# Gate and up rows of an expert side by side in one slot, multiplied as 512 columns

## What is computed

```python
def hier_moe(h, w_rg, b_rg, w_re, b_re, w1, w3, w2):
    """Top-1 group, then top-2 experts inside the chosen group; weight = p_group * p_expert."""
...
    comb = jnp.sum(jax.nn.one_hot(eid, N_EXPERTS, dtype=jnp.float32) * wts[..., None], axis=1)
    act = jax.nn.silu(jnp.einsum("nd,edf->nef", xt, w1)) * jnp.einsum("nd,edf->nef", xt, w3)
    act = act * comb[:, :, None].astype(act.dtype)
    y = jnp.einsum("nef,efd->nd", act, w2)
    return y.reshape(bsz, s, d)
```

## Time and profile before

| | |
|---|---|
| time, median of 3 runs (lowest to highest) | 917.99 us (917.68 to 918.61) |
| span of the profiled execution, first to last instruction | 914.1 us |
| PE (matmul) busy | 877.1 us, 96% |
| PEld (weight load) busy | 814.0 us, 89% |
| DVE busy | 625.9 us, 68% |
| ACT busy | 482.0 us, 53% |
| chain that ended last | PE 80%, DVE 13%, ACT 4% |
| HBM traffic over the span | 170 GB/s |

### The profile page before, as it was taken

The page is one execution under the profiler, slowest core; times in us unless marked ns, Lnnn a source line. Parts: engine busy times, 40 slices in busy tenths (PEclk is TensorE's granted clock), DMA queues, the critical chain, the costliest instruction groups (busy, mean ns, idle before and its releaser), DMA issues.

```text
span 914.1 us, 16487 instructions
## 1 busy us (share of the span) xinstructions
PE 877.1 (96%) x7196; PEld 814.0 (89%) x7196; DVE 625.9 (68%) x755; ACT 482.0 (53%) x576; POOL 44.5 (5%) x66
## 2 busy tenths in 40 slices
PE   5999999998988999999999999989999999999997
PEld 4998898998878999999979788989989999999986
DVE  5979477698938855478885986995466555455564
ACT  6557713657426744367774744565545543443463
POOL 6000060000000000000000000131000000000000
PEclk9999999999988999999999999999999999999999
DMA  9746210423107974579954544351454665555521
GB/s 268 264 157 203 88 49 4 139 93 139 47 1 301 380 272 162 187 269 365 356 195 139 184 139 138 98 191 51 169 184 150 211 204 184 184 185 186 183 92 46
DMA packets 88889, 156.73 MB, mean 171 GB/s; under 512 B 7417, under 2 KB 61169, under 8 KB 84849
## 3 DMA queue, kind: packets, MB, share of 16 engines
q1 hardware_dynamic: 88272, 155.42, 49.1%
q10 hardware_dynamic: 544, 0.26, 0.1%
HBM read 154.62 MB, written 1.05 MB: 170 GB/s over the span
## 4 chain that ended last, share of the span: by engine, by line
PE 80%; DVE 13%; ACT 4%; issue 2%; DMA 1%; POOL 0%; SPq 0%; DVEq 0%; POOLq 0%
PE ps L1043 9%; PE ps L1046 9%; PE ps L1045 9%; PE ps L1061 8%; PE ps L1063 8%; PE ps L1062 8%; DVE w_lo L1777 4%; PE ps L1485 4%; PE ps L1483 4%; PE ps L1484 4%; PE ps L1251 3%; PE ps L1555 2%; PE ps L1557 2%; PE ps L1556 2%; ACT w_hi L559 2%
## 5 line engine op out<-in xcount | busy, mean ns | idle before, releaser
L1777 DVE TENSOR_TENSOR w_lo<-raw,w_hi 128x2048 fp32r<-128x2048 f32 (+2 forms) x147 | 334.3, 2280 | 139.3 <-ACT w_hi L559 138.1
L559 ACT ACTIVATE w_hi<-raw 128x2048 fp32r<-128x2048 f32 (+2 forms) x147 | 277.5, 1892 | 76.4 <-PE ps L1063 27.5
L1043 PE MATMUL ps<-h_hi,w_hi 128*128 128x256 f32 x768 | 219.6, 286 | 5.9 <-DVE h_lo L1787 3.3
L1045 PE MATMUL ps<-h_lo,w_hi 128*128 128x256 f32 x768 | 217.2, 283 | 0.0
L1046 PE MATMUL ps<-h_hi,w_lo 128*128 128x256 f32 x768 | 217.2, 283 | 0.0
L1043 PEld LDWEIGHTS ps<-h_hi,w_hi 128*128 128x128 f32 x768 | 147.1, 192 | 8.7 <-issue 3.9
L1045 PEld LDWEIGHTS ps<-h_lo,w_hi 128*128 128x128 f32 x768 | 147.2, 192 | 0.4
L1046 PEld LDWEIGHTS ps<-h_hi,w_lo 128*128 128x128 f32 x768 | 147.1, 192 | 0.0
L1061 PE MATMUL ps<-w_hi,h_hi 128*128 128x512 f32 (+1 forms) x240 | 94.5, 394 | 0.5 <-DVE h_lo L2183 0.5
L1063 PE MATMUL ps<-w_hi,h_lo 128*128 128x512 f32 (+1 forms) x240 | 93.3, 389 | 0.0
L1062 PE MATMUL ps<-w_lo,h_hi 128*128 128x512 f32 (+1 forms) x240 | 93.2, 388 | 0.0
(11 more groups left out here) (435 smaller groups left out, 1350.5 us busy)
## 6 DMA issues: line engine op xcount, KB each, us to landing
raw<-in_w_in SPq DMA_DIRECT2D x36, 1024.0 KB, 5.1
raw<-in_w_exp_up SPq DMA_DIRECT2D x16, 1024.0 KB, 4.9
raw<-in_w_exp_down SPq DMA_DIRECT2D x16, 1024.0 KB, 4.9
raw<-in_w_exp_gate SPq DMA_DIRECT2D x15, 1024.0 KB, 4.9
raw<-in_w_ffn_gate SPq DMA_DIRECT2D x11, 1024.0 KB, 5.2
raw<-in_w_ffn_up SPq DMA_DIRECT2D x11, 1024.0 KB, 5.2
raw<-in_w_ffn_down SPq DMA_DIRECT2D x11, 1024.0 KB, 4.8
raw<-in_w_out SPq DMA_DIRECT2D x8, 1024.0 KB, 5.0
```

The costliest lines, as they stand in the source:

```text
L559: act.activation(w_hi[:, j % SPL, 0:kt * n], raw[:, j % RAW, 0:kt * n], ACT.Copy).then_inc(w_high, 1)
L1043: pe.matmul(o, hi[:, k, cols], a_hi[:, k, :], start=(k == 0 and (whole or c == 0)), stop=False)
L1045: pe.matmul(o, hi[:, k, cols], a_lo[:, k, :], start=False, stop=False)
L1777: dve.tensor_tensor(w_lo[:, j % SPL, 0:kt * n], raw[:, j % RAW, 0:kt * n], w_hi[:, j % SPL, 0:kt * n].bitcast(F32), sub).then_inc(w_ready, 1)
```

## The change

Gate and up rows of the same k are loaded next to each other: a chunk is `[128, k, 512]` with gate in columns 0 to 255 and up in 256 to 511, loaded by two DMAs into one slot. An expert's 8 k come as two chunks of 4 k each (expert 0: four chunks of 2 k), so there are still two full chunks for an expert and one for its down. TensorE multiplies 512 columns at a time into one bank for each set of tokens, first half of k for all sets, transposes of s - 1, second half. Silu reads columns 0 to 255 of the bank and the product columns 256 to 511, both after the second half. The calls of `ahead` on ACT and DVE are placed anew.

```diff
-        EXP[0][0] = add(first_rows(0, 0), (KD // 2, D_EXP))
-        FIRST = EXP[0][0]
-        add(first_rows(0, 1), (KD // 2, D_EXP))
-        EXP[0][1] = add(expert(w_exp_up, 0, "(p k) n -> p k n"), (KD, D_EXP))
+        def gate_and_up(s, ks):
+            gate_rows, up_rows = (expert(w, s, "(p k) n -> p k n") for w in (w_exp_gate, w_exp_up))
+            GATE_UP[s].append(add(lambda group: [(slice(D_EXP * j, D_EXP * j + D_EXP), rows(group)[:, ks, :])
+                                                 for j, rows in enumerate((gate_rows, up_rows))],
+                                  (ks.stop - ks.start, 2 * D_EXP)))
...
+        for q in range(4):
+            gate_and_up(0, slice(2 * q, 2 * q + 2))
         for s in range(1, N_EXP):
-            EXP[s][0] = add(expert(w_exp_gate, s, "(p k) n -> p k n"), (KD, D_EXP))
-            EXP[s][1] = add(expert(w_exp_up, s, "(p k) n -> p k n"), (KD, D_EXP))
-            down_chunk(s - 1)
-        down_chunk(N_EXP - 1)
+            for half in range(2):
+                gate_and_up(s, slice(4 * half, 4 * half + 4))
+            down_rows(s - 1)
+        down_rows(N_EXP - 1)
+        FIRST, LAST = GATE_UP[0][0], DOWN[N_EXP - 1]
...
-                sp.dma_start(dst, src).then_inc(w_in_sem[slot], 16)
+                for cols, rows_in in parts:
+                    sp.dma_start(dst[:, :, cols], rows_in).then_inc(w_in_sem[slot], 16)
...
@@ ACT, routing @@
-                ahead(FIRST + 4 - SPL)
+                ahead(FIRST + 6 - SPL)
...
@@ ACT, sparse_experts @@
                 for s in range(N_EXP):
                     if s:
-                        ahead(EXP[s][0])
-                    act.wait_ge(w_used, EXP[s][1])
+                        act_high_of(s - 1)
+                        ahead(GATE_UP[s][0] + 1, LAST + 1)
+                    act.wait_ge(w_used, GATE_UP[s][-1] + 1)
...
-                    if s:
-                        act_high_of(s - 1)
-                    ahead(EXP[s][1])
-                    if s:
-                        ahead(EXP[s - 1][2])
+                    if s + 1 < N_EXP:
+                        ahead(GATE_UP[s + 1][1] + 1 - SPL)
+                        ahead(DOWN[s] + 1 - SPL)
...
+                ahead(LAST + 1 - SPL)
                 act_high_of(N_EXP - 1)
                 act.wait_ge(s_sp_ps, PS_LAST_DOWN)
                 slots_out_high(1, 0)
-                act.wait_ge(w_used, EXP[N_EXP - 1][2] + 1)
+                act.wait_ge(w_used, LAST + 1)
                 slots_out_high(1, 1)
-                ahead(EXP[N_EXP - 1][2])
+                ahead(LAST)
...
@@ TensorE, sparse_experts @@
+                    outs = [(toks[w], bank(4 + 2 * (s % 2) + n)) for n, w in enumerate(WINDOWS[s // PER_GROUP])]
+                    k0 = 0
+                    for part, i in enumerate(GATE_UP[s]):
+                        ks = range(k0, k0 + chunks[i][1])
+                        tokens_still(i, outs, ks, (lambda k: pe.wait_ge(s_xs, k + 1)) if s == 0 else (lambda k: None))
+                        k0 = ks.stop
+                        if s and part == 0:
+                            turn_act(s - 1)
                     if s == 0:
                         slot_tiles()
                     else:
-                        tokens_still(EXP[s][0], gate_out)
-                        turn_act(s - 1)
-                    tokens_still(EXP[s][1], up_out)
-                    if s:
                         down(s - 1, range(2), w_used)
...
@@ DVE, sparse_experts @@
                     if s:
-                        ahead(EXP[s][0])
                         act_low_of(s - 1)
-                        ahead(EXP[s][1])
-                    else:
-                        ahead(FIRST + 4 - SPL)
-                    dve.wait_ge(w_used, EXP[s][1] + 1)
+                        ahead(GATE_UP[s][0] + 1, LAST + 1)
+                    dve.wait_ge(w_used, GATE_UP[s][-1] + 1)
...
-                    if s:
-                        ahead(EXP[s - 1][2])
+                    if s + 1 < N_EXP:
+                        ahead(GATE_UP[s + 1][1] + 1 - SPL)
+                        ahead(DOWN[s] + 1 - SPL)
...
+                ahead(LAST + 1 - SPL)
                 act_low_of(N_EXP - 1)
...
@@ DVE, ahead of the slots' scalars @@
-            ahead(FIRST + 3 - SPL)
+            ahead(FIRST + 6 - SPL)
             dve.wait_ge(s_sp_ps, PS_SCAL)
             dve.tensor_copy(slot_scal, split3(bank(0)[:, 0:34], 2)).then_inc(s_sl, 1)
```

More of the change, by code:

```diff
@@ L114, in expert, with down_rows @@
                 "o " + by_rows.replace("->", "-> o"), p=P)[0]
[L116 to L124, removed]
-        EXP[0][0] = add(first_rows(0, 0), (KD // 2, D_EXP))
-        FIRST = EXP[0][0]
-        add(first_rows(0, 1), (KD // 2, D_EXP))
-        EXP[0][1] = add(expert(w_exp_up, 0, "(p k) n -> p k n"), (KD, D_EXP))
-        for s in range(1, N_EXP):
-            EXP[s][0] = add(expert(w_exp_gate, s, "(p k) n -> p k n"), (KD, D_EXP))
-            EXP[s][1] = add(expert(w_exp_up, s, "(p k) n -> p k n"), (KD, D_EXP))
-            down_chunk(s - 1)
-        down_chunk(N_EXP - 1)
+        GATE_UP = [[] for _ in range(N_EXP)]
+        DOWN = []
+        def gate_and_up(s, ks):
[3 more added lines that the diff above has]
+                                  (ks.stop - ks.start, 2 * D_EXP)))
+        def down_rows(s):
+            rows = expert(w_exp_down, s, "(k p) n -> p k n")
+            DOWN.append(add(lambda group: [(slice(0, DM), rows(group))], (D_EXP // P, DM)))
+        for q in range(4):
+            gate_and_up(0, slice(2 * q, 2 * q + 2))
+        for s in range(1, N_EXP):
+            for half in range(2):
[3 more added lines that the diff above has]
+        FIRST, LAST = GATE_UP[0][0], DOWN[N_EXP - 1]
         HGQF = [add(rows_by(wi2, slice(256 * c, 256 * c + 256))) for c in range(4)]
@@ L156, in two_block_program, with landed @@
         N_CH = len(chunks)
+        TWO_PARTS = [i for parts in GATE_UP for i in parts]
+        def landed(i):
+            return 16 * sum(2 if j in TWO_PARTS else 1 for j in range(i % RAW, i + 1, RAW))
         LVL2 = [TOK2[1 + n // 2][n % 2] for n in range(8)]
@@ L463, in _ @@
                 for pos in range(N_GROUPS):
-                    if i == EXP[PER_GROUP * pos][0]:
+                    if i == GATE_UP[PER_GROUP * pos][0]:
                         group[pos] = sp.value_load(order_i[0:1, pos:pos + 1], min_val=0, max_val=N_EXP - PER_GROUP)
-                if FIRST <= i <= EXP[N_EXP - 1][2]:
-                    src = src(group)
+                parts = src(group) if FIRST <= i <= LAST else [(slice(0, n), src)]
                 if i >= RAW:
@@ L1473, in turn_cols, with tokens_still @@
                 m.then_inc(sig, 1)
-            def tokens_still(i, outs, ks=range(KD), ready=lambda k: None):
+            def tokens_still(i, outs, ks, ready):
                 hi, lo = chunk(i)
@@ L1546, in down @@
                     pe.wait_ge(s_sp_act, SB_PLACE_T)
-                hi, lo = chunk(EXP[s][2])
+                hi, lo = chunk(DOWN[s])
                 b = 2 * (s % 2)
@@ L1570, in sparse_experts @@
                 for s in range(N_EXP):
-                    wins = WINDOWS[s // PER_GROUP]
-                    gate_out, up_out = ([(toks[w], bank(b + 2 * (s % 2))[:, D_EXP * n:D_EXP * n + D_EXP])
-                                         for n, w in enumerate(wins)] for b in (4, 5))
+                    outs = [(toks[w], bank(4 + 2 * (s % 2) + n)) for n, w in enumerate(WINDOWS[s // PER_GROUP])]
[6 more added lines that the diff above has]
+                            turn_act(s - 1)
                     if s == 0:
-                        tokens_still(FIRST, gate_out, range(0, 4), lambda k: pe.wait_ge(s_xs, k + 1))
-                        tokens_still(FIRST + 1, gate_out, range(4, 8), lambda k: pe.wait_ge(s_xs, k + 1))
                         slot_tiles()
                     else:
-                        tokens_still(EXP[s][0], gate_out)
-                        turn_act(s - 1)
-                    tokens_still(EXP[s][1], up_out)
-                    if s:
                         down(s - 1, range(2), w_used)
@@ L2269, in sparse_experts @@
                         m = dve.scalar_tensor_tensor(act_p2[:, s % 2, n],
-                                                     bank(5 + 2 * (s % 2))[:, D_EXP * n:D_EXP * n + D_EXP],
+                                                     bank(4 + 2 * (s % 2) + n)[:, D_EXP:2 * D_EXP],
                                                      slot_scal[:, w, s:][:, 0:1],
```

6 lines of the change are left out of this document (3 added, 3 removed).

## The result

| | before | after |
|---|---|---|
| median (lowest to highest), 4 runs each | 917.84 us (916.36 to 918.61) | 925.38 us (924.38 to 925.69) |
| ratio, 95% interval | 1 | 1.0083 (1.0069 to 1.0098) |
| profiled execution: span | 914.1 us | 923.4 us |
| PE busy, chain of PE / DVE / ACT | 877.1 us, 80 / 13 / 4% | 877.3 us, 71 / 16 / 6% |

The change costs 7.5 us (6.3 to 9.0 by the interval). PE's busy time is the same, as the page of after shows, but its share of the chain that ended last fell by nine points. What grew are the shares of DVE, ACT and the DMAs (4% where it was 1%): more time is spent waiting for them.

A forecast was written before the change was run, and what follows sets the result against it. TensorE was taken as the bound from 280 to 460 us. Span 914.1 + 2.5 (start) - 4.9 (matmuls) + 0.6 (expert 9) + 4.4 (hand-over) + 1.8 (clock) = 918.5, so median 917.99 + 4.4 = 922.4 us, range 919.2 to 926.2.

The forecast's parts named there:

- hand-over: Experts to next layer: that layer's first chunk is split later on ACT and DVE, so TensorE starts later, +4.4 us.
- clock behind it: Behind the hand-over: TensorE's 5.6 us of idle time drops its clock to about half for a stretch, +1.8 us.
- start: Experts 0 and 1: less is loaded ahead and scalars wait behind a later chunk, +2.5 us (+1.5 to +3.8).
- wide matmuls: Gate and up of experts 2 to 15: 24 wide matmuls replace 48 narrow ones, 0.27 us less each time, -4.9 us.
- pauses between the experts: At expert 9, two takes of results delay the low half of the activation, +0.6 us (0 to 0.9).
- Rivals C and D: C: after the hand-over's idle the clock holds, 920.6 us, chance 0.13; D: hand-over costs nothing, 916.2 us, chance 0.07.
- the same step of two widths can be read side by side: Experts: 48 narrow matmuls at 5.75 us compared with 24 wide ones of a down at 5.48, giving 0.27 us less.
- leaves each chunk 0.8 to 1.2 us early: Experts' steady state: with silu behind up, ACT and DVE still prepare chunks in time, costed at nothing.
- the 0 for the smaller pieces: Experts' weight loads: 1 KB DMA pieces leave no slack, but transfers can run ahead, so costed at 0.
- rival B: One-set experts: the DMA engines become the bound, 0.39 us per expert, 3.9 us for ten, 926.3 us; chance 0.13.
- Rival E: Experts: wide matmuls save nothing, for instance because each weight load is exposed, about 927 us; chance 0.05.
- they land at 289.7 and ... at 292.7: Start: expert 1's two chunks land at these times, the first 5.1 us after issue, the second 2.95 us later.

The follow-up runs named there:

- e1: Changed kernel, but DVE and ACT split the next layer's first chunk behind the last expert's silu and product, inside the experts' loop: 921.06 us, ratio 1.0038.
- e2: Kernel before, with only the split of the next layer's first chunk kept out of the experts' loop on ACT and DVE: 923.51 us, ratio 1.0066.
- e5: Changed kernel with 36 unused matmuls of 256 columns put into TensorE's idle gap ahead of the next layer: 924.44 us, ratio 1.007.
- e9: Changed kernel with the gathered tokens (stationary operand of gate and up) in h_hi and h_lo instead of the arena: 923.28 us in one run.
- e4: Changed kernel with gate and up one behind the other in a slot, 4 KB pieces instead of 1 KB, still two DMAs per chunk: 926.1 us, ratio 1.0086.
- e7: Changed kernel with the early split of the next layer's first chunk and 4 KB pieces together: 920.06 us, ratio 1.0027.
- e3: Kernel before, with full gate and up chunks each loaded by two DMAs in 1 KB pieces, as in the change: 918.88 us, ratio 1.002.
- e6: Changed kernel with expert 0 loaded in three parts instead of four, so 3 MB is loaded ahead: 925.54 us, ratio 1.0076.
- e12: Changed kernel with early split, expert 0 in three parts and slot tiles ahead of its last part, keeping 1 KB pieces: 920.72 us, ratio 1.004.
- e11: Changed kernel with early split, 4 KB pieces, expert 0 in three parts and slot tiles ahead of its last part: 920.63 us, ratio 1.0037.
- e8: Changed kernel with early split, 4 KB pieces and expert 0 in three parts together: 920.1 us, ratio 1.0022.

## Why the prediction was right in its sum and where its steps failed

The forecast was 922.4 us in 919.2 to 926.2, slower; measured 925.38. By steps, forecast against measured:

| step | forecast | measured |
|---|---|---|
| hand-over | +4.4 | +4.16 |
| clock behind it | +1.8 | +1.80 |
| start | +2.5 (1.5 to 3.8) | +3.83 |
| wide matmuls | -4.9 | -2.7 |
| pauses between the experts | +0.6 | +1.8 |

**Hand-over and clock: right.** The order on DVE and ACT was read from the code, the times from the earlier trace rows, and e1, e2 and e5 showed each part by itself. Rivals C and D, the clock holds or the hand-over is free, are out. In the profiled executions about half of the 1.80 us came back further on, where before's clock fell and after's didn't.

**Wide matmuls: mechanism right, size wrong.** The step that failed is "the same step of two widths can be read side by side". It can't: the wide rows were down's, with another stationary operand. In their own place 24 wide matmuls take 5.60 us against 5.75 for 48 narrow ones, 0.15 for a set and not 0.27: 10 x 0.15 + 4 x 0.30 = 2.7 us, 2.2 less than forecast. e9 is the evidence that the difference between 5.60 and the 5.48 that I had read comes from the place of the operand, and not from the width: it has 5.44 there.

The Trainium skill (TensorE: Matmul & The Clock Gate, "Wait — 56ns, not 53.3ns?") has a matmul at its columns over 2.4 GHz plus about 2.5 ns, which gives 215.8 ns for 512 columns. After's rows have 233 and e9's 227 (256 columns: 120, where the page would have 109). So the trace agrees in neither, and the pitch differs by the place, of which the page's sum knows nothing. By that page the forecast would have been 3.8 us higher, nearer to the result, for a reason that the rows don't bear out.

**Pauses: too small.** The steps that failed are "leaves each chunk 0.8 to 1.2 us early" and the 0 for the smaller pieces, both costed at nothing. The experts' stage got only 0.9 us shorter in all, so 2.7 - 0.9 = 1.8 us went into waits that I had put at 0.6, at expert 9. The one-set experts at the end show them: PE of after, and what ACT waited for between 402 and 464 us (total us, count, longest).

```profile
437.71 0.50 PE L1491 MATMUL ps<-w_hi,arena_rounded 128*128 128x512 f32 x1 [0.49 <-DVE w_lo L1784]
```

```profile
ACT w_hi L567 <- DMA raw<-in_w_exp_down: 4.4, 5, 1.3
ACT w_hi L567 <- DMA raw<-in_w_exp_up: 3.5, 6, 1.3
```

ACT waited eleven times for chunks in flight, where before it waited for none in that stretch, and now and then the low part behind it came too late for PE. Read from one gate to the next, the one-set experts from 402.35 us on take 8.57, 8.96, 8.59, 9.24, 8.83 and 8.57 us in after; in e1, from 401.32 us, 8.57, 8.95, 8.59, 8.60, 8.57 and 8.54; before each took 8.72. So the undisturbed length is 8.57 (8.45 was forecast). The pause at expert 9 is +0.4 where I had +0.6, in both. The others, +0.7 and +0.3, and +0.4 in the last expert (455.11 to 464.06), come in after and not in e1; the two differ in no instruction up to the product of expert 15. That looks like rival B in the small: the load of the DMA engines as near to TensorE's as I had worked out, with no slack left. It is argued from ACT's waits and not shown by an edit. B's 3.9 us was not paid, and the piece size which it blamed is not seen in the stage: e4 has 4 KB and no shorter experts (156.15 against 156.04), e7 none either (154.96 against 154.62). What decides whether a pause comes is open; the later landing of down is the nearest candidate, and not shown. By itself it is not enough, since e3 has it (6.9 us), its ACT waits for chunks of the experts eight times in that stretch, and its one-set experts don't pause there. Rival E, wide matmuls save nothing, is out with the 8.57.

The Trainium skill (DMA: Bandwidth & Descriptors, "Specifications") has about 358 GB/s as the memory side's limit for a core, by which each of these experts would take at least 8.8 us. The mean of the six is 8.79 in after but 8.64 in e1, and the earlier trace rows has 370: close by, but not a floor in these runs.

**Start: right way, the landings too early.** The steps that failed are "they land at 289.7 and ... at 292.7", 4.3 and 7.3 us behind the first gate. ACT and DVE of after:

```profile
292.32 1.92 ACT L567 ACTIVATE w_hi<-raw 128x2048 fp32r<-128x2048 f32 x1 [2.77 <-DMA raw<-in_w_exp_up]
295.75 1.91 ACT L567 ACTIVATE w_hi<-raw 128x2048 fp32r<-128x2048 f32 x1 [1.51 <-DMA raw<-in_w_exp_up]
298.16 1.28 ACT L900 ACT_TABLE_LOAD   x1
300.12 0.47 ACT L900 ACTIVATE arena<-ps,small 128x256 f32<-128x256 f32 x1 [0.68 <-DVE small L2381]
...
299.90 0.18 DVE L2381 COPY small<-ps 128x34 f32<-128x34 f32 x1
```

The copies begin 5.67 and 9.10 us behind the first gate (286.65), so 1.4 and 1.8 later than forecast, and everything behind them moves along: scalars' copy, silu, product. I had taken the 5.1 us of a single DMA of 1 KB pieces, where each chunk comes by two, behind the last parts of expert 0. The chain behind the landings held: the scalars' copy waits for both low parts, silu for the copy, and the table load lies under the wait, as forecast. The sum landed at the upper bound of its range.

On PE the start shows as four waits: 1.26 us at the third quarter of expert 0, 0.89 at the first half of expert 1, 1.59 for the product of expert 0 and 0.60 for the low half of its activation. That is 4.34 us where before had one of 0.64, so +3.70 of the +3.83. The last three stand behind the late landings. The first doesn't: DVE begins that quarter's low part at 290.10, straight behind other work of its own. The number of parts is a piece of it (1.34 us, e6). The piece size may be another (1.26 us in e4, 0.45 in e7, nothing from e12 to e11), and the two don't add up (e8 has both mends, and 20.00). The move of the slot tiles behind up, which I had costed at nothing, takes away what filled PE's wait at the last part of expert 0: 2.33 us of idle PE in e8, and 0.64 in e11, which has them ahead.

**The sum: inside the range, partly by luck.** The three misses have one sign: +2.2, +1.2 and +1.3 us. Against them stands 0.2 at the hand-over, so the stretches have +8.9 us where the forecast had +4.4. The medians have less, 925.38 against the 917.99 from which I had started, +7.4. Of the 1.5 us between, 0.86 can be the second fall of the clock, which before's profile shows and after's doesn't; I had taken everything behind the first 24 matmuls as unchanged. How often the unprofiled executions had it is not known. The other 0.6 us is open and inside the interval. So the median is 3.0 us over the forecast. With all of +8.9 it would have been 926.9, outside the range. The 3.9 us between span and median, which I had called launch and end, are some 2 us of those and 2 us by which the profiled execution was faster than its median; the forecast adds its terms to the median, so this did no harm.

None of the kernels with the change beat the one before: the nearest, e7 and e8, are 2.1 us slower and e1, e11 and e12 3 us, and most of what they lose lies in the start.

## What to carry to other kernels

An engine's busy time says little about an edit whose gain is 3 us in a stage of 157: look at the two ends of the stage, at what waits there, and at every call that the edit moves in an in-order engine's program, since 4.2 us more of waiting came from the last call of a prefetch in the loop, which stops one chunk sooner than before. Take a matmul's pitch from rows with the same operands in the same place, not from rows of the same width alone. And when the work behind a product is merged with it, count what independent work used to stand between the parts: it was filling a wait.

## What the runs showed of the hardware that I had not expected

- The pitch of 512-column matmuls was 0.233 us with the stationary operand in one place of the on-chip memory and 0.227 in another (after and e9, 24 matmuls each: 5.60 and 5.44 us), 3% for a place.
- With two DMAs of 512 KB in place of one of 1 MB (and pieces of 4 or 1 KB in place of 8 KB), the chunk behind them, issued at the same distance as before (2.6 us behind up in e3), landed after 6.9 to 7.0 us where it took 4.9 (e3, e4, after).
- A stop of PE for 5.3 us cost 1.8 us more in what followed (4.78 for 2.98 us), while 36 useless matmuls in the gap kept the clock up behind it. The length of a stop alone does not say what follows: the clock fell behind stops of 2.69 us (e11, a stretch at 0.56) and of 1.85 us (e9, at 300.6 us, with stops of 1.27 and 0.89 us in the 10 us ahead of it), and it did not behind 2.33 us (e6, e8) or 1.17 us (e1).
- A second fall of the clock, between 505 and 520 us, comes in some kernels' profiled executions and not in others', and goes with 0.9 us in the rest of the span (441.2 against 440.3 us), more than several of the edits here are worth.
